# The first embedding layer's input products computed in the attention stage and kept in SBUF

## The reference

```python
def first_block(x, p, positions, norm_g, ple_w_gate, ple_w_proj, ...):
    h = x
    for i in range(DEPTH):
        hn = rmsnorm(h, norm_g[i])
        j = i // 2
        if i % 2 == 0:
            m = even_layer(hn, i, positions, ...)
        ...
        h = h + m
        h = h + jax.nn.sigmoid(h @ ple_w_gate[i]) * (p[i] @ ple_w_proj[i])
    return h
```

## Time and profile before

| what | us |
|---|---|
| median of 3 runs | 2598.07 (2596.12 to 2600.13) |
| the profiled execution's own time | 2599.05 |
| its span in the profile | 2597.1 |
| attention stage, 199.0 to 278.7 | 79.7 |
| output product, 278.7 to 328.7 | 50.0 |
| embedding layer, 328.7 to 407.0 | 78.3 |

### The profile page before, as it was taken

The page is one execution under the profiler, slowest core; times in us unless marked ns, Lnnn a source line. Parts: engine busy times, 40 slices in busy tenths (PEclk is TensorE's granted clock), DMA queues, the critical chain, the costliest instruction groups (busy, mean ns, idle before and its releaser), DMA issues. The chain is left out here.

```text
span 2597.1 us, 38108 instructions
## 1 busy us (share of the span) xinstructions
PE 2459.3 (95%) x15294; PEld 1353.5 (52%) x15294; DVE 1093.4 (42%) x2094; ACT 626.1 (24%) x1451; POOL 648.0 (25%) x753
## 2 busy tenths in 40 slices
PE   8997899989989999999999899989999899999998
PEld 5554445846544444555445445458555455454543
DVE  4636553554155554764212111264666641111113
ACT  2217113333211221732001000032455121000100
POOL 1734343462124231440000000120354200000001
PEclk9998999999999999999999999989999899999999
DMA  5521013110120411154999999951101359999998
GB/s 192 196 88 49 33 37 130 50 39 3 36 81 10 156 66 66 50 214 171 387 426 426 426 425 426 423 204 65 34 35 66 133 231 425 426 426 427 426 426 346
DMA packets 118651, 537.28 MB, mean 207 GB/s; under 512 B 24688, under 2 KB 40048, under 8 KB 85744
## 3 DMA queue, kind: packets, MB, share of 16 engines
q1 hardware_dynamic: 110624, 516.23, 49.6%
q0 software_dynamic: 7888, 19.14, 2.0%
HBM read 509.89 MB, written 33.06 MB: 209 GB/s over the span
## 5 line engine op out<-in xcount | busy, mean ns | idle before, releaser
L3961 PE MATMUL psum<-arena,hidden_T 128*64 128x512 f32 x1376 | 303.0, 592 | 0.0
L3973 PE MATMUL psum<-weight_ring,hidden_T 128*64 128x512 f32 x1024 | 239.1, 610 | 18.9 <-DMA weight_ring<-in_moe_w_down 18.0
L3939 PEld LDWEIGHTS psum<-hidden_T,arena 128*128 128x128 f32 x1904 | 220.4, 192 | 43.4 <-issue 43.4
L3939 PE MATMUL psum<-hidden_T,arena 128*128 128x128 f32 x1904 | 234.5, 278 | 1.2 <-DVE hidden_T L3934 1.2
L3961 PEld LDWEIGHTS psum<-arena,hidden_T 128*64 128x64 f32 x1376 | 100.5, 137 | 193.3 <-issue 193.1
L4216 ACT ACTIVATE hidden_T<-psum 128x256 f32<-128x256 f32 x64 | 24.5, 383 | 708.0 <-PE psum L3961 708.0
L3961 PE MATMUL psum<-weight_ring,hidden_T 128*64 128x512 f32 x672 | 149.2, 594 | 0.0
L3955 DVE TENSOR_TENSOR hidden_T<-psum,norm_gains 128x512 f32<-128x512 f32 x64 | 43.8, 691 | 248.8 <-PE psum L3961 153.2
L3973 PEld LDWEIGHTS psum<-weight_ring,hidden_T 128*64 128x64 f32 x1024 | 71.0, 139 | 143.7 <-issue 134.9
L4009 POOL DMA_INDIRECT expert_rows_out<-hidden_T,small x30 | 29.7, 990 | 462.9 <-DVE hidden_T L4315 409.4
L4009 POOL DMA_INDIRECT expert_rows_out<-arena,small x30 | 29.8, 992 | 386.7 <-DVE arena L4315 345.2
(11 more groups left out here) (663 smaller groups left out, 4439.4 us busy)
## 6 DMA issues: line engine op xcount, KB each, us to landing
arena<-in_moe_w_up SPq DMA_DIRECT2D x86, 2048.0 KB, 22.7
weight_ring<-in_moe_w_down SPq DMA_DIRECT2D x64, 2048.0 KB, 21.0
weight_ring<-in_moe_w_up SPq DMA_DIRECT2D x42, 2048.0 KB, 22.1
weight_ring<-in_hg_w_in SPq DMA_DIRECT2D x8, 2048.0 KB, 10.9
weight_ring<-in_ev_w_in SPq DMA_DIRECT2D x8, 1536.0 KB, 9.4
weight_ring<-in_fox_w_in SPq DMA_DIRECT2D x6, 2048.0 KB, 12.0
weight_ring<-in_od_w_in SPq DMA_DIRECT2D x5, 2048.0 KB, 8.2
weight_ring<-in_ple_w_gate SPq DMA_DIRECT2D x4, 2048.0 KB, 9.0
```

The source lines that it names most:

```text
L3939: last = nc.tensor.matmul(g.psum[:, c // 4, (c % 4) * P:(c % 4 + 1) * P], keep[:, i, c * P:(c + 1) * P], row[:, i, :], start=i == 0, stop= ...
L3961: last = nc.tensor.matmul(g.psum[64 * q:64 * q + 64, 2 + n, :].rearrange("p (s c) -> p s c", s=2), xT[:, k // 4, k % 4, ROWS * n:ROWS * n ...
L3973: last = nc.tensor.matmul(g.psum[64 * q:64 * q + 64, 6 + n, :], aT[:, k % 2, 64 * (k // 2):64 * (k // 2) + 64], down[b][:, k, 512 * q:512 ...
```

## The change

The eight input products leave `stage_ple` of the first layer and are made in the attention, as `project(q, k)`, where k is one of the two matmuls. The table `pieces` sets their steps: q = 0 is split over steps 4 and 5, q = 1 to 5 stand whole in steps 7, 9, 11, 13 and 18, q = 6 is split over 24 and 25, and q = 7 over 30 and 31. All go to bank 7. Between product and next product DVE copies the bank to SBUF (`park`), one step later, after `peaks`. `proj_order` says which block each q is; four of the parked blocks stand where the pooling's inputs and gates were, and four where its sums were, all of which are free after the pooling.

The inputs `p` are loaded in the attention, as four loads of 128 columns, into parts of `hidden_T` that the attention's own rows fill later; so from q = 5 on a product also waits until rows have been placed, which frees bank 7 too. The row transposes of tile t wait for product 4 + t to be copied. SP issues the `proj` weights first, then the four loads, then the gate chunk. The embedding layer drops `pT`, its load and `project`; its multiply reads two SBUF operands; its order changes. `stage_out` and `stage_ple` get fixed scratch places around the parked blocks. The second embedding layer, with `parked` None, is as before.

```diff
+PAIRS_OF_TILES = [(1, 2), (3, 4)]
+PLE_BLOCKS = [(0, 2, 0, 0), (1, 2, 0, 0), (0, 7, 1, 1), (0, 3, 0, 1), (0, 4, 1, 0), (1, 7, 1, 1), (1, 3, 0, 1), (1, 4, 1, 0)]
...
+    if parked:
+        steps = [("turn", "raw", 1), ("turn", "raw", 2), (1, 0), ("turn", "raw", 3), (2, 0), ("turn", "raw", 4), (1, 1), (6, 0), (2, 1), (5, 0), (7, 0), (3, 0), (4, 0)]
+        steps += [(6, 1), (5, 1), (7, 1), ("turn", "norm", 1), (3, 1), (4, 1), ("turn", "norm", 2), ("turn", "norm", 3), ("turn", "norm", 4)]
...
-                dve.wait_ge(*proj_ready.at(e + 1))
-                nc.vector.tensor_tensor(gates[:, e, :], gates[:, e, :], bank(4 + e % 2), ALU.mult).then_inc(*multiplied.up())
+                if not parked:
+                    dve.wait_ge(*proj_ready.at(e + 1))
+                nc.vector.tensor_tensor(gates[:, e, :], gates[:, e, :], parked.proj[e] if parked else bank(4 + e % 2), ALU.mult).then_inc(*multiplied.up())
...
-                    if p and n == 5:
+                    if p and n == (7 if parked else 5):
                         move("norm", 1)
-                    if p and n == 7:
+                    if p and n == (4 if parked else 7):
                         move("norm", 2)
...
+    proj_order = [5, 7, 0, 1, 2, 3, 4, 6]
+    pieces = {4: [(0, 0)], 5: [(0, 1)], 24: [(6, 0)], 25: [(6, 1)], 30: [(7, 0)], 31: [(7, 1)]}
+    pieces.update({j: [(q, 0), (q, 1)] for q, j in ((1, 7), (2, 9), (3, 11), (4, 13), (5, 18))})
...
             def turn_rows(t, half):
                 pe.wait_ge(*rows_ready.at(t + 1))
+                if half == 0:
+                    pe.wait_ge(*proj_taken.at(5 + t))
...
+            def project(q, k):
+                p, _, i, half = PLE_BLOCKS[proj_order[q]]
+                if (q, k) == (0, 0):
+                    g.weights_wait(pe, proj_chunk)
+                    pe.wait_ge(*p_in.at(64))
+                    pe.wait_ge(*pooling.done.at(2))
+                if q and k == 0:
+                    pe.wait_ge(*proj_taken.at(q))
+                if q > 4 and k == 0:
+                    pe.wait_ge(*rows_placed.at(2 * (q - 4)))
+                last = nc.tensor.matmul(g.psum[:, 7, :], input_block(PAIRS_OF_TILES[p][i] - 1, k), g.weights(proj_chunk)[:, k, 512 * half:512 * half + 512], start=k == 0, stop=k == 1)
+                if k:
+                    last.then_inc(*proj_ready.up())
...
                 if j < N:
                     scores(j)
+                for q, k in pieces.get(j, []):
+                    project(q, k)
...
         def _(sp):
+            g.feed(sp, proj_chunk + 1)
+            for t in range(4):
+                at = 2 + 2 * t % 6
+                sp.dma_start(g.hT[:, at:at + 2, META + P * (3 - 2 * t // 6):META + P * (4 - 2 * t // 6)], g.a["p_T"][0][:, P * t:P * t + P].rearrange("(k p) t -> p k t", p=P)).then_inc(*p_in.up(16))
             g.feed(sp, ring_upto)
...
+            def park(q):
+                dve.wait_ge(*proj_ready.at(q + 1))
+                v.tensor_copy(parked.proj[proj_order[q]], g.psum[:, 7, :]).then_inc(*proj_taken.up())
...
                     peaks(j)
+                for q, k in pieces.get(j - 1, []):
+                    if k:
+                        park(q)
                 if 1 <= j < N + 1:
                     invert(j - 1)
```

More of the change, by code:

```diff
@@ L584, in stage_out, with stage_ple @@
     g.top = mark
-def stage_ple(g, layer, chunks, proj_chunk, tiles, gain, ring_upto):
+PAIRS_OF_TILES = [(1, 2), (3, 4)]
+PLE_BLOCKS = [(0, 2, 0, 0), (1, 2, 0, 0), (0, 7, 1, 1), (0, 3, 0, 1), (0, 4, 1, 0), (1, 7, 1, 1), (1, 3, 0, 1), (1, 4, 1, 0)]
+Parked = namedtuple("Parked", "proj square out_scratch low high")
+def stage_ple(g, layer, chunks, proj_chunk, tiles, gain, ring_upto, parked=None):
     nc = g.nc
@@ L594, in stage_ple @@
     copied, taken, summed, weighted = g.sig("values_copied", "bank_read_by_vector", "block_sums_ready", "weight_sums_ready")
-    pT = g.take(2, SEQ)
+    pT = None if parked else g.take(2, SEQ)
+    if parked:
+        g.top = parked.low
     T = [g.take(4, 512) for _ in range(4)]
     S = [[g.take(4, P) for _ in range(4)] for _ in range(2)]
+    if parked:
+        g.top = parked.high
     first, gates = g.take(2, 512), g.take(8, 512)
-    sq, rows = g.take(D), g.take(2, D)
+    sq, rows = parked.square if parked else g.take(D), g.take(2, D)
     ss, rs = g.take(5), g.take(5)
     few = [0] if 0 in tiles else []
-    pairs = [(1, 2), (3, 4)]
+    pairs = PAIRS_OF_TILES
     operands = [block_products(row_blocks(g.hT, pair), weight_blocks(g, chunks), S[p], T) for p, pair in enumerate(pairs)]
@@ L611, in stage_ple @@
     nth = {t: i for i, t in enumerate(few + list(XT))}
-    blocks = [(0, 2, 0, 0), (1, 2, 0, 0), (0, 7, 1, 1), (0, 3, 0, 1), (0, 4, 1, 0), (1, 7, 1, 1), (1, 3, 0, 1), (1, 4, 1, 0)]
+    blocks = PLE_BLOCKS
     block_at = {block[:2]: e for e, block in enumerate(blocks)}
@@ L691, in _ @@
                         g.chunk_used(chunks[1], ready)
-            g.chunk_used(proj_chunk, proj_ready)
+            if not parked:
+                g.chunk_used(proj_chunk, proj_ready)
         @block.sync
         def _(sp):
-            sp.dma_start(pT, g.a["p_T"][layer].rearrange("(k p) t -> p k t", p=P)).then_inc(*p_in.up(16))
+            if not parked:
+                sp.dma_start(pT, g.a["p_T"][layer].rearrange("(k p) t -> p k t", p=P)).then_inc(*p_in.up(16))
             g.feed(sp, ring_upto)
@@ L1292, in __init__ @@
         self.s = g.take(2, 2, 16 + SEQ)
+        self.end = g.top
         self.factors = g.take(2, SEQ)
@@ L1347, in gate, with park_products, stage_even_attention @@
             g.nc.vector.scalar_tensor_tensor(g.hT[:, n, META:], g.psum[:, 5 + 2 * n, :], self.scale[:, n:n + 1], g.e_gate[:, n, :], ALU.mult, ALU.mult).then_inc(*self.done.up())
-def stage_even_attention(g, ring_upto):
+def park_products(g):
+    low, high = 2 * (16 + SEQ) + 2 * SEQ, g.pooling.end
+    first, second = g.arena[:, 0:4 * 512], g.pooling.s.rearrange("p a b n -> p (a b n)")
+    grid = lambda ap, e: ap[:, 512 * e:512 * e + 512]
+    proj = [grid(first, e) for e in range(4)] + [grid(second, e) for e in range(4)]
+    scratch = (g.arena[:, low:low + 8192], g.arena[:, low + 8192:low + 12288], g.arena[:, high:high + 1024], None)
+    return Parked(proj, g.arena[:, 0:D], scratch, low, high)
+def stage_even_attention(g, ring_upto, proj_chunk, parked):
     nc = g.nc
@@ L1358, in stage_even_attention @@
     weighted = g.sig("values_copied")
+    p_in, proj_ready, proj_taken = g.sig("inputs_loaded", "product_ready", "bank_read_by_vector")
     strip = g.small[:, 512:1024]
@@ L5257, in build @@
         stage_even_in(g, even, even_out[0] + 2)
-        stage_even_attention(g, even_out[0] + 4)
-        g.top = 0
-        stage_out(g, XT, even_out, even_out[1] + 4)
+        parked = park_products(g)
         gate, proj = plans["ple0"]
-        stage_ple(g, 0, gate, proj, XT, g.gain(1), plans["odd"][0][0] + 4)
+        stage_even_attention(g, even_out[0] + 4, proj, parked)
+        stage_out(g, XT, even_out, even_out[1] + 4, None, parked.out_scratch)
+        stage_ple(g, 0, gate, proj, XT, g.gain(1), plans["odd"][0][0] + 4, parked)
         odd_layer(g, plans["odd"])
```

3 lines of the change are left out of this document (added).

## The result

The changed kernel took 2587.68 us (median of 9, 2582.14 to 2591.11), the kernel before 2598.32 (9 runs, 2591.29 to 2603.53): a ratio of 0.995 with a 95% interval of 0.9937 to 0.9964. That is faster by about 11 us where 7 were forecast. Repeated twice beside the experiments, the same pair gave 0.9972 (0.9958 to 0.9987; 2589.97 against 2597.21) and 0.9967 (0.9953 to 0.998; 2588.13 against 2595.82), so 7 to 9 us.

A forecast was written before the change was run, and what follows sets the result against it. PE was taken to bound the embedding layer, while the attention was a pipeline of waits. 12.8 us gained less 5.5 lost gave 7.3, so 2591.8 from 2599.05, forecast as a 2591 us median; range 2586 to 2598.

The forecast's parts named there:

- the tail of the embedding layer: Embedding layer behind block product (4, 1): the shorter multiply wait and ACT's later square cancel; zero, 0.5 us either way.
- the last step: Whole kernel: net 7.3 us taken off the profiled execution's 2599.05, giving 2591.8; the median 1.0 below that, so 2591.
- Seven products off PE's line, (6, 0) in the gap, the transposes behind (4, 1), a wait of 0.95: Embedding layer on PE: 12.04 + 0.78 + 0.88 - 0.95 = 12.75, say 12.8 us gained.
- Rival D: Embedding layer: block products wait for DVE, at most four more waits of about 0.95 us; 2595 us, chance 0.05.
- The multiply with two SBUF operands, zero: Embedding layer on DVE: a multiply may be held by one of POOL's adds; counted zero, upper bound 1 us.
- Loads, 0.3: Attention, first product: wait for the input loads between 0 and 3.3 us, taken as 0.3 lost.
- Rival C: Attention, step 4: inputs land late, near 209.7, and PE stands 3 us more; 2594 us, chance 0.10.
- q = 4, 0.6 of 0.3 to 1.6: Attention: row transposes wait 1.6 us longer for DVE's copy, partly hidden by ACT; 0.3 to 1.6 lost, 0.6 taken.
- The attention's sum before the clock, 6.9: Attention's added work and waits: 0.3 + 0.4 + 2.4 + 0.6 + 1.0 + 2.2 = 6.9 us lost.
- The clock, 1.4 of 2.6 given back: Attention: new matmuls fill gaps where the clock fell; 1.6 and about 1.0 us possible, 1.4 counted, leaving 5.5 lost.
- A: Attention: clock falls as before, q = 1 to 3 cost 10.3 us instead of 2.4; 2600 us, chance 0.12.
- B: Attention: low clock reaches the whole stage and its tail, 8.6 us more than A; slower, 2609 us, chance 0.05.

## Why the prediction came out as it did

Faster was right and the time lies inside the range, but the forecast of 7.3 us was too small for the 10.6 of the first comparison. That it is close to the 7.2 and 7.7 of the repeats is luck: the three stages gave 6.4 against the same execution of before, out of terms that were off by up to 2 us each way. Two steps failed: the tail of the embedding layer, counted at nothing, cost 2.0 us; and the last step, which put the stages' sum on one execution of before and so took the stages behind as equal, where the profiled executions differ by 8.0 us there. By its steps:

- **Seven products off PE's line, (6, 0) in the gap, the transposes behind (4, 1), a wait of 0.95.** The end of (4, 1) moved from 67.79 us after the stage's start to 54.99 (388.48 less 333.49): 12.80 against 12.75. The wait is 0.87. Rival D is false, no other block product waits.
- **The tail, counted at nothing with 0.5 either way.** This is the step of the sum that failed. From the end of (4, 1) the tail grew by 2.0 us, from 9.64 to 11.65. I followed DVE, ACT and POOL through it, and there the sum was good: ACT's last scaling starts 5.75 us behind (4, 1) where it started 6.14 behind it. I did not follow PE. The eighth product is gone from the tail and only tile 2's transposes, half as long, stand in its place; ACT's scaling of tile 3 comes 0.7 us later. So PE is idle for 2.31 us where it was idle for 0.76, the clock falls, and the holding matmuls behind cost 1.60 more. Where the clock stays up the layer is 64.95, and the tail costs 0.3, by the four matmuls in a row: with them split the tail is 0.4 shorter than before, not longer.
- **The multiply with two SBUF operands, zero.** Right, 0.69 us in all eight. The bound of 1 us wasn't needed.
- **The output product, which the sum leaves out.** It gained 1.04 us, by the scratch's place.
- **Loads, 0.3.** No wait shows: `project` for q = 0 began at 205.77. The four input loads landed 4.9 us after issue. Rival C is false.
- **q = 4, 0.6 of 0.3 to 1.6.** Right, for the reason given. The row transposes start 1.66 us later for the copy (forecast 1.6), and ACT hides about 1.0 of that: with the copy moved PE waits 1.28 us for ACT behind them, and tile 1 starts only 0.67 sooner.
- **The attention's sum before the clock, 6.9.** Against the execution of before with a full clock in tile 1 it is 7.9 (84.80 less 76.89). Up to the first row transposes the pipeline lost 5.2 us (34.83 from the stage's start against 29.67), between these and tile 1's 0.4, up to tile 2's 0.7 and up to the last ones 1.7. Set beside the kernel with the two copies moved, this parts as follows: q = 0 to 3 cost 3.5 (forecast 3.1), q = 4 0.7 (0.6), q = 5 1.4 (1.0), q = 6's copy 0.7 and q = 7 1.7, together 2.3 (2.2). So 0.4 each was missing at q = 0 to 3 and at q = 5, PE's own steps among the scores. It is an estimate from one execution of each kernel, in which the second fall of the clock does not lie at quite the same place.
- **The clock, 1.4 of 2.6 given back.** Against the profiled execution 2.5 came back, all in tile 1, where 1.6 was the most that I had reckoned for it. The second fall stayed, so neither "all of it" nor "as before" (A, B) was right. The Trainium skill (TensorE: Matmul & The Clock Gate, What's actually happening) has activity release the clock. Tile 1 of the changed kernel agrees, with PE busy 15.36 of 16.45 us at 1.00, and so does the fall behind it, where PE first stands for 3.46 us. But the kernel before stood at 0.53 with PE busy 12.95 of 13.61 us in one execution and at 1.00 with 9.93 in the other, so the rule by itself does not tell which executions fall.

So the attention's 5.4 (5.5 forecast) is right by luck, because its cost was 1.0 too small and the clock's return 1.1 too small. The total's error has two sources. In the stages the tail lost 2.0 us, and the output product gave back 1.0. Around them I took one execution of before as the kernel's own, with its clock: the kernel before has executions from 2588.72 to 2605.45 us, and a median of three says little about a difference of 7. The term of the clock should have been a range by itself, as wide as the fall that one execution shows and another doesn't, 2.5 us, and the total should have had one of its own for the stages behind.

## What to carry to other kernels

Work that is taken off the engine that sets the clock leaves a hole: look at the end of a stage for what that engine does in the time won, since two holding matmuls on either side of the gap were 2.4 us better here than the same four in a row behind it. A copy that frees something another engine waits for belongs ahead of the long instructions of its queue, not behind them; but what a shorter wait is worth is read further on, where the next engine may be waited for (here 1.66 us of wait gave 0.7 us, and the two copies together 1.3). And where a fall of the clock comes in one execution and not in the next, stages should be compared by their rows, and totals by several executions beside their mean clock.

## What the runs showed of the hardware

- The granted clock differs between executions of one kernel, at one and the same place (0.53 and 1.00 over 13.6 us). Over 84 executions the time follows the mean clock with 1.6 us for each 0.001.
- A kernel with 16 matmuls more, in the pipeline's thin places, was 0.2% faster (2591.22 against 2594.81 us), at a mean clock of 0.983 to 0.989.
- After one and the same gap of 2.3 us on PE the clock fell in four of six executions and stayed up in two.
- A GpSimd addition of two SBUF operands of 128x512 takes 2.19 or 2.37 us (13.15 / 6 and 14.19 / 6) beside the same work of VectorE, by where one of its operands stands. VectorE's sums at the same time were shorter with it: 3.18 instead of 3.36 us. What it is in the place I don't know; only these places were tried.
